# Runs of four gathers from one table in place of alternating single gathers

## The reference

```python
def peer(h, w_pq, sub_keys, u_tab, v_tab):          # for a block of 128 tokens
    q = (xb @ w_pq).reshape(128, 8, 2, 128)
    s = einsum('thpd,hpnd->thpn', q, sub_keys)       # scores against 2 x 128 keys
    ...                                              # top 16 of the 256 sums of the two top 16
    u = take(u_tab, expert, axis=0)                  # per token and head: 16 rows of 1024
    v = take(v_tab, expert, axis=0)
    a = gelu(einsum('td,thkd->thk', xb, u)) * g
    return einsum('thk,thkd->td', a, v)
```

## Time and profile before

| | |
|---|---|
| runs | 5337.58, 5336.59, 5332.83 us; median 5336.59 |
| profiled execution, span from first to last instruction | 5334.1 us |
| TensorE busy (matmul) | 4580.5 us, 86% |
| VectorE busy | 2976.1 us, 56% |
| GpSimd busy | 2427.7 us, 46% |
| ScalarE busy | 1065.3 us, 20% |
| DMA | 1506.39 MB, mean 282 GB/s; 1342.34 MB of it on the queue of GpSimd's gathers |

### The profile page before, as it was taken

The page is one execution under the profiler, slowest core; times in us unless marked ns, Lnnn a source line. Parts: engine busy times, 40 slices in busy tenths (PEclk is TensorE's granted clock), DMA queues, the critical chain, the costliest instruction groups (busy, mean ns, idle before and its releaser), DMA issues.

```text
span 5334.1 us, 50012 instructions
## 1 busy us (share of the span) xinstructions
PE 4580.5 (86%) x14880; PEld 2248.8 (42%) x14880; DVE 2976.1 (56%) x7190; ACT 1065.3 (20%) x2651; POOL 2427.7 (46%) x2576
## 2 busy tenths in 40 slices
PE   4999899978888888888888778899986888888887
PEld 2466655533333333333333333555443333333333
DVE  1554411167676776767766634552137677676764
ACT  0123300012222222222222111231002222222221
POOL 0000000017777777777776540000006777777775
PEclk7999799989999999999999988999998999999999
DMA  7000011339999999999999991000249999999998
GB/s 292 0 20 28 0 42 52 115 115 413 419 416 418 419 408 420 408 415 419 418 419 421 420 392 43 16 31 31 76 160 366 419 413 416 419 411 419 415 419 350
DMA packets 391232, 1506.39 MB, mean 282 GB/s; under 512 B 44408, under 2 KB 45048, under 8 KB 386936
## 3 DMA queue, kind: packets, MB, share of 16 engines
q0 software_dynamic: 368640, 1342.34, 62.0%
q1 hardware_dynamic: 22392, 161.72, 8.0%
HBM read 1501.69 MB, written 2.20 MB: 282 GB/s over the span
## 4 chain that ended last, share of the span: by engine, by line
PE 37%; issue 20%; DMA 20%; POOL 16%; DVE 7%; ACT 1%; SPq 0%; POOLq 0%; DVEq 0%; ACTq 0%
PE ps L480 34%; DMA arena<-in_u_tab,idx 17%; POOL arena L449 8%; POOL arena L459 8%; DVE arena L1310 3%; DMA arena<-in_v_tab,idx 2%; PE ps L587 2%; DMA arena<-in_w_mod 1%; DMA arena<-in_w_qkv 0%; ACT arena L785 0%; DVE arena L1132 0%; DVE mx L1118 0%; DMA mods<-arena 0%; PE ps L512 0%; DVE arena L1243 0%
## 5 line engine op out<-in xcount | busy, mean ns | idle before, releaser
L480 PE MATMUL ps<-arena 128*128 128x512 f32 (+7 forms) x12032 | 4373.1, 520 | 613.8 <-DMA arena<-in_v_tab,idx 416.2
L480 PEld LDWEIGHTS ps<-arena 128*128 128x128 f32 (+1 forms) x12032 | 2059.4, 196 | 2843.1 <-issue 1635.2
L449 POOL DMA_INDIRECT arena<-in_u_tab,idx x1280 | 1212.1, 947 | 2437.2 <-DVE idx L1387 1985.2
L1310 DVE CUSTOM_DVE_ANT_0 arena<-arena,ps 128x1024 f32<-128x1024 f32 x1280 | 1562.6, 1221 | 997.7 <-DMA arena<-in_u_tab,idx 996.3
L459 POOL DMA_INDIRECT arena<-in_v_tab,idx x1280 | 1212.2, 947 | 445.4 <-issue 363.0
L785 ACT COPY arena<-ps 128x256 f32<-128x256 f32 (+3 forms) x518 | 219.4, 429 | 1611.8 <-PE ps L480 881.6
L921 ACT ACTIVATE arena<-ident,coef 128x128 f32<-128x128 f32 x1280 | 382.5, 387 | 375.9 <-DVE coef L1317 375.9
L1236 DVE TENSOR_TENSOR arena<-arena,ps 128x768 f32<-128x768 f32 (+1 forms) x32 | 26.3, 822 | 370.3 <-PE ps L480 370.3
L941 ACT ACTIVATE gl<-dots 128x16 f32<-128x16 f32 x80 | 17.3, 216 | 1003.6 <-DVE dots L1310 1003.6
L1132 DVE COPY arena<-ps 128x384 f32<-128x384 f32 (+1 forms) x128 | 79.9, 624 | 216.3 <-PE ps L587 211.6
L853 ACT ACTIVATE arena<-ps,nm 128x768 f32<-128x768 f32 (+2 forms) x160 | 123.6, 772 | 289.7 <-DVE nm L1122 162.3
(11 more groups left out here) (111 smaller groups left out, 1627.0 us busy)
## 6 DMA issues: line engine op xcount, KB each, us to landing
arena<-in_w_mod SPq DMA_DIRECT2D x24, 2048.0 KB, 11.0
arena<-in_w_gb SPq DMA_DIRECT2D x48, 768.0 KB, 4.2
arena<-in_u_tab,idx POOLq DMA_INDIRECT x1280, 8.2
arena<-in_v_tab,idx POOLq DMA_INDIRECT x1280, 8.2
arena<-in_w_qkv SPq DMA_DIRECT2D x2, 6144.0 KB, 22.2
arena<-in_w_conv SPq DMA_DIRECT2D x24, 512.0 KB, 3.6
arena<-mods SPq DMA_DIRECT2D x21, 512.0 KB, 6.7
arena<-in_w_out SPq DMA_DIRECT2D x2, 4096.0 KB, 13.4
```

Of the source, the lines that this page charges most:

```text
L449: nc.gpsimd.indirect_dma_start(ur[:, row % UR, :], None, u_rows, bass.IndirectOffsetOnAxis(ap=idx[:, at:at + 1], axis=0)).then_inc(u_in[ro ...
L480: return nc.tensor.matmul(o, lhsT, rhs, start=first, stop=last, skip_group_check=True)
L1310: v.tensor_tensor_reduce(u, u, h_cur, 1.0, 0.0, ALU.mult, ALU.add, dots[:, i % 2, k:k + 1]).then_inc(s["dots_done"], 1)
```

## The change

GpSimd issues the gathers of four rows of u, then those of four rows of v, and so on. Each gather keeps its own wait, its slot and its semaphore; all other engines' programs are the same.

```diff
--- before.py
+++ after.py
@@ -42,6 +42,7 @@
 NK = 128
 EXPERTS = NK * NK
 UR, VR = 6, 8
+RUN = 4
 LAG = 2
 LEAD = 3
 
@@ -463,11 +464,13 @@
             for l in range(LAYERS):
                 i0, heads = PH * n_tiles[l], PH * live[l]
                 for i in range(heads + 1):
-                    for k in range(TOPK):
+                    for k0 in range(0, TOPK, RUN):
                         if i < heads:
-                            gather_u(i0 + i, k)
+                            for k in range(k0, k0 + RUN):
+                                gather_u(i0 + i, k)
                         if i > 0:
-                            gather_v(i0 + i - 1, k)
+                            for k in range(k0, k0 + RUN):
+                                gather_v(i0 + i - 1, k)
 
 
         @block.tensor
```

## The result

The changed kernel takes **5342.39 us** (median of 20 runs, 5334.64 to 5349.01), the kernel before 5333.36 us beside it (20 runs, 5329.32 to 5338.25). The ratio is 1.0016, with a 95% interval of 1.0009 to 1.0022: 8.5 us more, 4.8 to 11.7.

What follows compares the result with a forecast made beforehand. Gathers were taken as the bound, DMA at 419 GB/s and GpSimd's issue at one pace. Terms -13.0 + 1.4 + 3.0 = -8.6 us took the span from 5334.1 to 5325.5, forecast as 5328 us; range 5315 to 5343.

Steps and rivals of the forecast that it cites:

- (a): Second head of each new tile: GpSimd's wait at v(8t,8) for TensorE goes, worth -13.0 us (bounds 0 and 25 us).
- The lateness formula: At a tile's start, v(8t,8) is late by delay - 6.3 us; delay runs from u gather start to its dot.
- the six windows: Stretches of 20 or 30 us at tiles' starts, short of 419 GB/s by 13.0 us' worth of bytes in all.
- rival A: Tile-start waits were free, late gathers land in a row, only beginnings and ends cost: 5341 us; chance 0.18.
- (b): Six-slot u ring: a run's fourth u waits for a dot when the delay exceeds 10.7 us; cost 0.
- C: Last six heads of layer 0 starve beside modulation weight loads, DMA running dry: +22 us, 5350 us; chance 0.10.
- (c): Beginnings of the two PEER stages: u(1,1) to u(1,3) go at the dots' pace before v; +1.4 us in all.
- (d): Ends of the two PEER stages: the last v land in a lump, so TensorE's last rows start later; +3.0 us.
- B: Each tile-start wait counts at its full length, 25 us gained: 5316 us; chance 0.12.
- D: TensorE's clock falls to half speed in each lump, only the two ends pay, 4 us: 5332 us; chance 0.10.

Runs made afterwards that it cites:

- e3_early_read: Old gather order, VectorE reading the finished tile behind dot 1 instead of dot 3, against the kernel before: 5332.47 us, ratio 0.9998.
- e1_middle: Runs of four only in the middle heads of each stage, first two and last two heads alternating, against the kernel before: 5336.01 us, ratio 1.0006.
- e11: The changed kernel with runs of eight instead of four, still six slots for u, against the kernel before: 5575.05 us, ratio 1.0453.
- e12_ends_third: Runs of four only in the first two and last two heads of each stage, alternating elsewhere, against the kernel before: 5338.71 us, ratio 1.0009.

## Why the prediction was wrong, by its own steps

**(a), the tile's wait: the mechanism right, the worth wrong. This is the step that failed.** The lateness formula fits the other tiles of before too (layer 1's v(16,8): a delay of 10.91 makes 4.6 us; the trace has 4.96 with the usual 0.3), the wait is gone, and the six windows show 406 to 419 GB/s. But the sentence "I take the bytes: -13.0 us" took a shortfall of bytes in a window for lost time. e3_early_read gives the shortfall back and gains 1.1 us (a gain of 5.9 to a loss of 3.7). Its lower bound, 0, was rival A's: the late gathers land in a row. The argument that I had noted for A, that the delay falls by about as much as GpSimd waits, was the one to follow: what the delay has above some 6 us is a reserve, a wait of 2 to 5 us draws on it, and the complete rows go on landing at 1.25 us. The landing rhythm across the stop was in the trace of before and would have said so. The missing bytes are those of engines that were ahead (the first counts lose 15.1 us, the last none). With the same step the prediction overrated the reserve in (b) and in C: of eight gathers outstanding some five are the time that a gather takes anyway.

**(b), the new condition on u: about 0, perhaps 3 us.** The waits came at the row that was named, the fourth u of a run, and where VectorE has extra work. e1_middle holds (a) and (b) together at +3.2 us (-1.6 to +8.0), and with (a) at -1.1 that leaves some 4 us for (b), though e1's interval still reaches below zero. That "GpSimd stands and the DMA engines don't" is not quite so: 371 and 359 GB/s around u(18,11). By the lesson of (a) this alone proves no loss, and the last counts say that there is none at this place: 27 gathers around it land in 33.57 us, 1.24 us each. Where the 3 us of the middle lie, if they are there at all, is not shown. e11 shows the price when the reserve is gone.

**(c) and (d), beginnings and ends: right.** 4.4 us were forecast; the kernel with them alone costs 5.9 and 4.8 us in two timings on the faster chips. (c) measured 0.95 and 0.89 us for 0.7 each; in (d) layer 1's tail runs 20 rows without a wait and is 1.5 us later, as drawn, and layer 0's 0 to 1.7.

**The rivals.** A (the waits were free, 5341) is what happened: 8.5 us measured against its 4.4, the rest of it small and, by e1_middle, in the middle. That its 5341 lies so near the 5342.39 is in part luck: it was reckoned from a median of three runs that lay 3.2 us above the 5333.36 of twenty. B (each wait counts in full) is excluded by the same runs. C (the last six heads of layer 0 starve, +22 us) didn't come: layer 0 is 1.1 us longer. D came, and cost nothing that can be seen. TensorE in the changed kernel, after an idle 3.51 us, and windows of 1 us and of 40 us:

```profile
1279.41 10.92 PE L483 MATMUL ps<-arena 128*128 128x512 f32 x21 [3.51 <-DMA arena<-in_v_tab,idx]
...
1281.00:1282.00 1.00, 1.00 (x2) 0.34 (x1) 0.13 (x1) 0.00 (x0) 0.82 (x1) 0.50 1.01 410
...
1350.00:1390.00 40.00, 36.59 (x95) 17.95 (x94) 26.18 (x72) 10.69 (x26) 30.22 (x33) 0.92 1.03 419
```

The window of the earlier trace rows had a clock of 1.00; in lumps it is 0.92, TensorE is busy 36.6 us of 40 in place of 35.4, and DMA is still at 419 GB/s. The mean granted clock fell from 0.956 to 0.935 (0.936 in e1_middle, 0.957 in e12_ends_third, so it is the middle's lumps). The rule of the Trainium skill that I cited for this (TensorE: Matmul & The Clock Gate, the section on HAM oscillation) agrees with the trace, now also for lumps between two DMA waits; it says what happens to the clock. Why the time doesn't feel it is the prediction's argument, not tested by a run of its own: a lump at the low clock was reckoned at 8.9 of 9.9 us, so it still fits. The tail ran at the pace of before (1.73 us a row), so D's 4 us at the ends didn't come.

## What to carry to other kernels

Where an engine issues ahead into a queue, price its wait by what lands: follow the landings across the stop. A window with fewer bytes is no lost time as long as complete transfers keep their rhythm; a wait costs when the time from issue to landing is down to what one transfer takes with nothing ahead of it. Here reordering transfers of equal size gained nothing, as the engine that was behind never ran out of work, and it cost at both ends of each stage, where a run makes the consumer wait for its whole length. Keep the run well below the number of slots: four of six cost 0.16%, eight of six 4.5%.

## What the runs showed of the hardware

- GpSimd's issue of a 128-row gather (1.24 to 1.25 us) bounds the quiet stretches level with the DMA engines: with a quarter of the gathered bytes left out, layer 1's gathers took 1277.97 us for 1276.83, and DMA stood at 309 to 315 GB/s.
- The parts of one gather land apart: the last of its 16 counts came 5.21 us after the first where the queue was long (issue to landing 12.76 us) and 0.84 us after it where a stop had emptied it (6.21 us). A rate in GB/s is a mean over engines, of which the last alone decides when a row is complete.
- The same kernel took 5333 to 5334 us on three occasions and 5791.69 us on another chip, where the gathers moved at some 360 GB/s instead of 419. There runs of eight cost 1.0065 instead of 1.0453. Probably that is because GpSimd, at 1.24 us, is faster than the DMA engines there and fills the queue again after each wait; this was not tested. What makes the gathers slower there is open.
